# One subtraction of 2048 columns for a weight chunk's low part, in place of two of 1024

## The chip, the cores and the metric

The kernel runs on one core of a Trainium2 chip. The metric is device time in microseconds (us) of that core. Three runs of the kernel before took 1616.21, 1616.61 and 1618.96 us, median 1616.61 us.

## The reference, cut to what matters

The program computes two stacked transformer blocks on one sequence of 256 tokens of width 1024, in float32. The first block has two layers (a hybrid attention mixer, then a differential attention mixer, each followed by a convolutional gated feed-forward network). The second block has two layers, each with a three-part mixer and a mixture of 32 experts (MoE) in four groups. Nearly all work is products with weights that are each used once:

```
def conv_glu_ffn(n, w_up, conv_w, conv_b, w_down):
    gate, up = jnp.split(n @ w_up, 2, axis=-1)
    ...
    return (jax.nn.silu(conv) * up) @ w_down

def hier_moe(h, ...):
    ...
    for g in range(N_GROUPS):
        a = jnp.einsum('nd,edf->nef', t, w_gate[g])
        b = jnp.einsum('nd,edf->nef', t, w_up[g])
        hid = jax.nn.silu(a) * b * combine[:, g, :, None]
        y = y + jnp.einsum('nef,efd->nd', hid, w_down[g])
```

## The kernel before, in words

All weights come from memory as one stream of 315 chunks. A chunk is 128 partitions by 2048 float32 columns, 1 MB, and three ring places (`RING = 3`) hold it in three forms: `raw` as it arrived, `w_high` (written by ScalarE, ACT, as a rounded copy of type float32r) and `w_low` (written by VectorE, DVE, as `raw - w_high`). TensorE (PE) makes each product from three passes: high by high, high by low, low by high (lines 1225 to 1227). So every chunk goes through four hands:

- SyncE (SP) issues the transfer of chunk c into `raw` once `w_low` of chunk c-3 is finished (line 259, 260), since both ScalarE and VectorE read `raw`.
- ScalarE's `split` (lines 337 to 350) waits for the transfer and for PE to be done with chunk c-3, whose `w_high` it overwrites. Then it copies the chunk in two halves of 1024 columns, line 347, and raises `w_high_ready` after each.
- VectorE's `split` subtracts, line 701, in two halves, each behind the half of ScalarE's that it reads. After the second it raises `w_low_ready`.
- PE waits for `w_low_ready`, multiplies, and raises `chunk_used`.

Every engine works through its own list in a fixed order that is written out by hand. In the MoE (`moe`, `turn`) one expert takes three chunks: two for gate and up, one for down. VectorE's turn reads: split of the down chunk of expert e, low part of its hidden rows (line 976), split of the first up chunk of expert e+2, the hidden rows of expert e+1 (line 972), split of the second up chunk. PE's turn reads: first up chunk of e+1, two transposes of the hidden rows of e (line 1482), second up chunk, down chunk of e. PE begins the first up chunk of the next expert only when line 972 has read the bank of the expert before. A group has eight experts. At its start PE also clears sums and scatters the last group's result, and in two turns of the first three groups it gathers the next group's tokens.

In the feed-forward network (`glu`) an up chunk holds moving tiles of 256 columns, and VectorE does for each of its tiles the convolution (lines 854, 857), the gating (860) and the low part (862), between the splits. At the end of the network VectorE splits one chunk ahead before it adds PE's four banks to the residual (`add_bank`, line 835).

Of the kernel before, what the change touches and what calls it, by code (L numbers as in the profile page):

```python
# [18 lines left out]
F32 = mybir.dt.float32  # L19
F32R = mybir.dt.float32r  # L20
ALU = mybir.AluOpType
# [17 lines left out]
CH = 2048  # L39
RING = 3  # L40
# [23 lines left out]
WIDTH = {C_FB: KT * 8}  # L64
# [47 lines left out]
def build(nc, x, stream, router, small, const, fgain, out):  # L112
    es = ExitStack()
    with es:
        def sb(name, shape, dt=F32):
            return es.enter_context(nc.sbuf_tensor(name, shape, dt))
# [4 lines left out]
        raw = sb("raw", [P, RING, CH])  # L121
        wh = sb("w_high", [P, RING, CH], F32R)
        wl = sb("w_low", [P, RING, CH], F32R)
# [74 lines left out]
        w_high, w_low, chunk_used = map(sem, ("w_high_ready", "w_low_ready", "chunk_used"))  # L198
# [484 lines left out]
        def _(dve):  # L683
            step = [0]
            tt, ts, stt = nc.vector.tensor_tensor, nc.vector.tensor_scalar, nc.vector.scalar_tensor_tensor
# [6 lines left out]
            def split(c, off=0):  # L692

                if isinstance(off, int) and c + RING * off >= NCHUNK:
                    return
                u = c % RING
                n = WIDTH.get(c, CH) // 2
                for half in range(2):
                    cols = slice(half * n, half * n + n)
                    dve.wait_ge(w_high, off * (2 * RING) + (2 * c + half + 1))  # L700
                    ins = tt(wl[:, u, cols], raw[:, u, cols], wh[:, u, cols].bitcast(F32), ALU.subtract)  # L701
                ins.then_inc(w_low, 1)

            def plain(c0, n):
                for c in range(c0, c0 + n):
                    split(c + AHEAD)
# [130 lines left out]
            def out_projection(c0):  # L837
                split(c0 + AHEAD)
                split(c0 + 1 + AHEAD)
                for half in range(2):  # L840
                    add_bank(0, half, None)
                    add_bank(1, half, c0 + 2 * half + 1)
                    if half == 0:
                        split(c0 + 2 + AHEAD)
# [279 lines left out]
            for l in range(LAYERS):  # L1124
                c0 = C_LAYER[l]
                n = 8 + 5 * l
# [822 lines left out]
```

## Time and profile before

| what | value |
|---|---|
| median of three runs | 1616.61 us (1616.21 to 1618.96) |
| span of the profiled execution | 1618.9 us, the same as the slowest of the three |
| PE busy | 1532.1 us (95%) |
| weight loads (PEld) | 1292.0 us (80%) |
| VectorE busy | 1139.9 us (70%) |
| ScalarE busy | 928.7 us (57%) |
| stream read | 335.5 MB, mean of all traffic 208 GB/s |
| mean granted TensorE clock | 0.959 of full speed |

Busy shares are averages over stages. The two MoE stages lie at about 855 to 1156 us and 1308 to 1609 us, the two feed-forward networks at about 180 to 374 us and 512 to 705 us.

### The profile page before, as it was taken

The page shows a single profiled execution, that of the slowest core. Times are in us where ns is not written, and L with a number is a line of the kernel's source. Part 1 is how long each engine was busy: PE and PEld are TensorE (multiplying, and loading weights), DVE is VectorE, ACT ScalarE, POOL GpSimd, SP SyncE. Part 2 cuts the span into 40 slices and gives each one's busy share as a digit, 9 for nine tenths or more (in the row PEclk, how much of TensorE's full clock was granted, in tenths as well). Part 3 has the DMA queues.
Part 4 walks back from the last instruction along what each step waited for, and adds up shares of the span by engine and source line. Part 5 has one row for each costly group of instructions (what it writes and reads, how often), then busy time and mean ns, then how long its engine had stood idle before and what let it go on. Part 6 is the DMA issues. An engine that isn't in the chain of part 4 may idle for free.

```text
span 1618.9 us, 23376 instructions
## 1 busy us (share of the span) xinstructions
PE 1532.1 (95%) x8148; PEld 1292.0 (80%) x8148; DVE 1139.9 (70%) x1869; ACT 928.7 (57%) x1522; POOL 32.6 (2%) x68
## 2 busy tenths in 40 slices
PE   7999999999989999989979999999899799999997
PEld 5877899997868999977768888887678678888875
DVE  6554566567686656665767889889755678888886
ACT  5432445445455545455536767676555367777764
POOL 0000000000010000010000000000000000000000
PEclk9986899999999999999989999999997899999999
DMA  8510354544413454442226989798530458898884
GB/s 323 183 52 27 131 184 179 194 188 161 174 37 114 179 202 181 181 160 104 82 102 251 353 309 357 296 363 336 221 140 21 162 195 331 322 355 314 336 331 192
DMA packets 46828, 336.77 MB, mean 208 GB/s; under 512 B 5344, under 2 KB 5472, under 8 KB 6432
## 3 DMA queue, kind: packets, MB, share of 16 engines
q1 hardware_dynamic: 46656, 335.49, 54.8%
q8 instruction: 44, 0.72, 0.2%
q0 software_dynamic: 96, 0.30, 0.1%
q14 instruction: 32, 0.26, 0.0%
HBM read 334.72 MB, written 1.05 MB: 207 GB/s over the span
## 4 chain that ended last, share of the span: by engine, by line
PE 86%; DVE 6%; ACT 4%; issue 2%; POOL 1%; DMA 1%; DVEq 0%; ACTq 0%; SPq 0%; POOLq 0%
PE bank L1225 23%; PE bank L1227 23%; PE bank L1226 23%; PE bank L1327 3%; DVE w_low L701 2%; PE bank L1439 2%; PE bank L1450 2%; PE bank L1337 1%; ACT w_high L347 1%; PE bank L1273 1%; PE bank L1482 1%; PE bank L1329 1%; PE bank L1284 1%; PE bank L1348 1%; PE bank L1347 1%
## 5 line engine op out<-in xcount | busy, mean ns | idle before, releaser
L701 DVE TENSOR_TENSOR w_low<-raw,w_high 128x1024 fp32r<-128x1024 f32 (+2 forms) x630 | 734.6, 1212 | 193.2 <-ACT w_high L347 190.9
L347 ACT ACTIVATE w_high<-raw 128x1024 fp32r<-128x1024 f32 (+2 forms) x630 | 623.5, 1044 | 106.2 <-PE bank L1227 69.5
L1225 PE MATMUL bank<-w_high,x_high 128*128 128x512 f32 (+1 forms) x928 | 375.9, 405 | 8.1 <-DVE rope_b L972 3.1
L1227 PE MATMUL bank<-w_high,x_low 128*128 128x512 f32 (+1 forms) x928 | 363.7, 392 | 0.0
L1226 PE MATMUL bank<-w_low,x_high 128*128 128x512 f32 (+1 forms) x928 | 361.6, 390 | 0.0
L1225 PEld LDWEIGHTS bank<-w_high,x_high 128*128 128x128 f32 x928 | 175.5, 189 | 46.8 <-issue 7.9
L1227 PEld LDWEIGHTS bank<-w_high,x_low 128*128 128x128 f32 x928 | 175.1, 189 | 38.1
L1225 PE MATMUL bank<-x_high,w_high 128*128 128x256 f32 (+1 forms) x712 | 203.2, 285 | 0.4 <-DVE rope_b L860 0.3
L1226 PEld LDWEIGHTS bank<-w_low,x_high 128*128 128x128 f32 x928 | 176.0, 190 | 34.1 <-issue 1.4
L1226 PE MATMUL bank<-x_low,w_high 128*128 128x256 f32 (+1 forms) x712 | 202.6, 285 | 0.0
L1227 PE MATMUL bank<-x_high,w_low 128*128 128x256 f32 (+1 forms) x712 | 202.5, 284 | 0.0
L1225 PE MATMUL bank<-w_high,hid_high 128*128 128x512 f32 x432 | 171.4, 397 | 1.9 <-DVE hid_low L976 1.9
L1226 PE MATMUL bank<-w_low,hid_high 128*128 128x512 f32 x432 | 170.5, 395 | 0.0
L1227 PE MATMUL bank<-w_high,hid_low 128*128 128x512 f32 x432 | 170.4, 394 | 0.0
L1225 PEld LDWEIGHTS bank<-x_high,w_high 128*128 128x128 f32 (+1 forms) x712 | 136.8, 192 | 2.6 <-issue 1.2
L1226 PEld LDWEIGHTS bank<-x_low,w_high 128*128 128x128 f32 (+1 forms) x712 | 136.8, 192 | 1.1
L1227 PEld LDWEIGHTS bank<-x_high,w_low 128*128 128x128 f32 (+1 forms) x712 | 136.8, 192 | 0.4
L1225 PEld LDWEIGHTS bank<-w_high,hid_high 128*128 128x128 f32 x432 | 81.4, 188 | 20.1 <-DVE hid_low L976 2.3
L1227 PEld LDWEIGHTS bank<-w_high,hid_low 128*128 128x128 f32 x432 | 81.4, 189 | 19.2
L1226 PEld LDWEIGHTS bank<-w_low,hid_high 128*128 128x128 f32 x432 | 81.5, 189 | 17.5
L393 ACT ACTIVATE probs<-scores_masked,neg_max 128x128 f32<-128x128 f32 x96 | 42.8, 446 | 82.0 <-DVE neg_max L760 81.9
L495 ACT ACTIVATE hid_high<-bank 128x256 fp32r<-128x256 f32 x64 | 24.5, 383 | 80.3 <-PE bank L1482 80.3
(235 smaller groups left out, 1477.3 us busy)
## 6 DMA issues: line engine op xcount, KB each, us to landing
raw<-stream SPq DMA_DIRECT2D x314, 1024.0 KB, 4.8
const_sb<-const SPq DMA_DIRECT2D x1, 2070.0 KB, 15.1
residual<-x SPq DMA_DIRECT2D x2, 512.0 KB, 4.0
final_gain<-fgain SPq DMA_DIRECT2D x2, 512.0 KB, 10.7
out<-residual SPq DMA_DIRECT2D x2, 512.0 KB, 2.6
small_sb<-small SPq DMA_DIRECT2D x1, 765.0 KB, 6.6
rope_a<-router POOLq DMA_DIRECT2D x2, 144.0 KB, 2.5
const_sb<-const SPq DMA_DIRECT2D x1, 136.0 KB, 4.3
```

The lines of the kernel that those rows point to most:

```text
L347: nc.scalar.activation(wh[:, u, cols], raw[:, u, cols], ACT.Copy).then_inc(w_high, 1)
L393: ins = nc.scalar.activation(pr[:, a % 2, lo:hi], sm[:, a % 2, lo:hi], ACT.Exp, bias=nmax[:, a, t:t + 1], scale=-1.0, accum_out=den[:, a, ...
L495: nc.scalar.activation(gh[:, 0, :, 0:P], B[6][:, 0:2 * P].rearrange("p (k s) -> p k s", k=2), ACT.Copy)\
L701: ins = tt(wl[:, u, cols], raw[:, u, cols], wh[:, u, cols].bitcast(F32), ALU.subtract)
L1225: mm(o, ah, bh, start=start, stop=False, **kw)
L1226: mm(o, ah, bl, start=False, stop=False, **kw)
L1227: return mm(o, al, bh, start=False, stop=stop, **kw)
L1273: ins = nc.tensor.transpose(B[4 + b][:, at:at + P], tok[:, t, k * P:(k + 1) * P], ident)
L1284: ins = nc.tensor.transpose(B[4 + b][:, at:at + P], src[:, t, k * P:(k + 1) * P], ident)
L1327: ins = mm(o[:, lo:hi], q[:, t * P:(t + 1) * P], k[:, 0:hi - lo], start=True, stop=f is None)
L1439: ins = mm(B[2 + b][:, (k % 4) * P:(k % 4 + 1) * P], tok[:, t, k * P:(k + 1) * P], pick[:, t, g, :], start=t == 0, stop=t == NT - 1)
L1450: ins = mm(B[((5, 7), (2, 3))[half][t]][:, :], spread[:, g, t * P:(t + 1) * P], ys[:, half * 512:(half + 1) * 512], start=True, stop=True)
```

## The change

VectorE's `split` issues one subtraction over all columns of the chunk, behind both of ScalarE's halves, where it had issued two, each behind one half.

```
             u = c % RING
-            n = WIDTH.get(c, CH) // 2
-            for half in range(2):
-                cols = slice(half * n, half * n + n)
-                dve.wait_ge(w_high, off * (2 * RING) + (2 * c + half + 1))
-                ins = tt(wl[:, u, cols], raw[:, u, cols], wh[:, u, cols].bitcast(F32), ALU.subtract)
-            ins.then_inc(w_low, 1)
+            n = WIDTH.get(c, CH)
+            dve.wait_ge(w_high, off * (2 * RING) + (2 * c + 2))
+            tt(wl[:, u, 0:n], raw[:, u, 0:n], wh[:, u, 0:n].bitcast(F32), ALU.subtract).then_inc(w_low, 1)
```

ScalarE, PE, GpSimd and SyncE keep their lists. On VectorE nothing changes place. Line numbers behind the edit fall by two or three (701 becomes 699, 972 becomes 969).

The body of the MoE loop on VectorE (`w_low<-raw,w_high` is the split, `hid_low` the low part of the hidden rows, `rope_b<-...combine` the hidden rows), before:

```order
L701 TENSOR_TENSOR w_low<-raw,w_high 128x1024 [waits w_high_ready]
L700 REGISTER_ALU
L701 TENSOR_TENSOR w_low<-raw,w_high 128x1024 [waits w_high_ready]
L975 REGISTER_ALU
L976 TENSOR_TENSOR hid_low<-bank,hid_high 128x2x128 [waits expert_high_ready]
L700 REGISTER_ALU
L701 TENSOR_TENSOR w_low<-raw,w_high 128x1024 [waits w_high_ready]
L700 REGISTER_ALU
L701 TENSOR_TENSOR w_low<-raw,w_high 128x1024 [waits w_high_ready]
L971 REGISTER_ALU
L972 ISA [waits expert_silu_ready]
L972 SCALAR_TENSOR_TENSOR rope_b<-rope_a,combine,bank 128x256
```

And now:

```order
L699 TENSOR_TENSOR w_low<-raw,w_high 128x2048 [waits w_high_ready]
L972 REGISTER_ALU
L973 TENSOR_TENSOR hid_low<-bank,hid_high 128x2x128 [waits expert_high_ready]
L698 REGISTER_ALU
L699 TENSOR_TENSOR w_low<-raw,w_high 128x2048 [waits w_high_ready]
L968 REGISTER_ALU
L969 ISA [waits expert_silu_ready]
L969 SCALAR_TENSOR_TENSOR rope_b<-rope_a,combine,bank 128x256
```

The order of the work is the same. One instruction with one wait stands where two with a wait each stood.

The end of a feed-forward network on VectorE (`residual<-residual,bank` are the four adds), before:

```order
L701 TENSOR_TENSOR w_low<-raw,w_high 128x1024 [waits w_high_ready]
L869 REGISTER_ALU
L869 COMPARE_AND_BRANCH
L701 TENSOR_TENSOR w_low<-raw,w_high 128x1024 [waits w_high_ready] x2
L835 TENSOR_TENSOR residual<-residual,bank 128x512 [waits bank_done] x3
```

And now:

```order
L699 TENSOR_TENSOR w_low<-raw,w_high 128x2048 [waits w_high_ready]
L866 REGISTER_ALU
L866 COMPARE_AND_BRANCH
L699 TENSOR_TENSOR w_low<-raw,w_high 128x2048 [waits w_high_ready]
L832 TENSOR_TENSOR residual<-residual,bank 128x512 [waits bank_done] x3
```

The adds stand behind two chunks' splits, as before.

## Rows read from the trace of the kernel before

**Rows 1.** The page: chain that ended last, shares by engine and line; ScalarE's split.
```profile
PE 86%; DVE 6%; ACT 4%; issue 2%; POOL 1%; DMA 1%; DVEq 0%; ACTq 0%; SPq 0%; POOLq 0%
PE bank L1225 23%; PE bank L1227 23%; PE bank L1226 23%; PE bank L1327 3%; DVE w_low L701 2%; PE bank L1439 2%; PE bank L1450 2%; PE bank L1337 1%; ACT w_high L347 1%; PE bank L1273 1%; PE bank L1482 1%; PE bank L1329 1%; PE bank L1284 1%; PE bank L1348 1%; PE bank L1347 1%
...
L347 ACT ACTIVATE w_high<-raw 128x1024 fp32r<-128x1024 f32 (+2 forms) x630 | 623.5, 1044 | 106.2 <-PE bank L1227 69.5
```

**Rows 2.** Busy time by stretch: a MoE group, feed-forward network, attention; columns are named.
```profile
core 0: us, PE busy (x) PEld busy (x) DVE busy (x) ACT busy (x) POOL busy (x), PEclk, DMA share, GB/s
1016.00:1092.00 76.00, 76.00 (x352) 61.33 (x352) 67.19 (x77) 55.36 (x75) 0.00 (x0) 1.00 0.87 333
...
270.00:300.00 30.00, 30.00 (x207) 27.88 (x206) 17.71 (x26) 15.24 (x23) 0.00 (x0) 1.00 0.52 192
...
106.00:150.00 44.00, 43.14 (x139) 30.54 (x138) 13.95 (x63) 7.37 (x29) 0.00 (x0) 0.50 0.00 0
```

**Rows 3.** VectorE's groups by shape: operation, shape, count | busy us, mean ns | idle before.
```profile
L701 DVE TENSOR_TENSOR w_low<-raw,w_high 128x1024 fp32r<-128x1024 f32 x620 | 728.3, 1221 | 190.8 <-ACT w_high L347 188.5
...
L701 DVE TENSOR_TENSOR w_low<-raw,w_high 128x768 fp32r<-128x768 f32 x4 | 3.7, 954 | 2.4 <-ACT w_high L347 2.4
```

**Rows 4.** ScalarE in order of time, MoE: start us, us, engine, line, operation.
```profile
1052.09 0.39 ACT L495 ACTIVATE hid_high<-bank 128x256 fp32r<-128x256 f32 x1 [0.96 <-PE bank L1482]
1052.42 2.01 ACT L347 ACTIVATE w_high<-raw 128x1024 fp32r<-128x1024 f32 x2
...
1060.91 2.00 ACT L347 ACTIVATE w_high<-raw 128x1024 fp32r<-128x1024 f32 x2
```

**Rows 5.** VectorE in order of time, the same stretch.
```profile
1044.93 2.36 DVE L701 TENSOR_TENSOR w_low<-raw,w_high 128x1024 fp32r<-128x1024 f32 x2 [0.52 <-ACT w_high L347]
...
1053.52 2.36 DVE L701 TENSOR_TENSOR w_low<-raw,w_high 128x1024 fp32r<-128x1024 f32 x2 [0.58 <-ACT w_high L347]
1055.80 0.47 DVE L972 SCALAR_TENSOR_TENSOR rope_b<-rope_a,combine,bank 128x256 f32<-128x256 f32 x1
...
1061.99 2.36 DVE L701 TENSOR_TENSOR w_low<-raw,w_high 128x1024 fp32r<-128x1024 f32 x2 [0.52 <-ACT w_high L347]
1064.27 0.47 DVE L972 SCALAR_TENSOR_TENSOR rope_b<-rope_a,combine,bank 128x256 f32<-128x256 f32 x1
```

**Rows 6.** SyncE's queue in order of time: issues behind two splits.
```profile
1037.11 0.33 SPq L260 DMA_DIRECT2D raw<-stream  x1
...
1056.05 0.33 SPq L260 DMA_DIRECT2D raw<-stream  x1
```

**Rows 7.** Transfers of 1050 to 1062 us: issues, KB each, median us to landing.
```profile
raw<-stream SPq DMA_DIRECT2D x5, 1024.0 KB, 4.8
```

**Rows 8.** PE in order of time: start of an expert's first up chunk.
```profile
1066.00 0.40 PE L1225 MATMUL bank<-w_high,x_high 128*128 128x512 f32 x1
```

**Rows 9.** VectorE in order of time, end of the first feed-forward network.
```profile
358.19 2.36 DVE L701 TENSOR_TENSOR w_low<-raw,w_high 128x1024 fp32r<-128x1024 f32 x2 [3.50 <-ACT w_high L347]
...
367.05 4.63 DVE L701 TENSOR_TENSOR w_low<-raw,w_high 128x1024 fp32r<-128x1024 f32 x4 [0.53 <-ACT w_high L347]
371.60 2.51 DVE L835 TENSOR_TENSOR residual<-residual,bank 128x512 f32<-128x512 f32 x4
```

**Rows 10.** Chain that ended last in order of time, whole run: start us, us, what.
```profile
15.54 2.37 DVE w_low L701 x2
...
192.35 2.36 DVE w_low L701 x2
...
731.72 2.36 DVE w_low L701 x2
...
793.92 2.36 DVE w_low L701 x2
...
827.40 4.63 DVE w_low L701 x4
...
1525.33 6.41 DMA raw<-stream
```

## The prediction, made before the changed kernel ran

> **What bounds the kernel now.** I read the chain of waits first. PE holds 86% of it, the three passes 69% [rows 1], and the rest is small pieces, among them 2% on VectorE's split. So a change on VectorE matters where PE waits for it, or where it starts something that PE will wait for. Next come the stretches [rows 2]. In a feed-forward network PE is busy all 30.00 us of 30 and VectorE 17.71: much room. In the MoE PE is busy all 76.00 us of 76, VectorE 67.19, and the transfers run at 0.87 of their capacity: PE is the bound, but nothing else is far behind. Last I follow one ring place through an MoE turn in order of time, which shows what stands just behind PE.
>
> **The cost of one split.** Both kernels do the same columns. A subtraction of 1024 columns takes 1221 ns, one of 768 takes 954 ns [rows 3]: (1221 - 954) / 256 = 1.04 ns a column, and a fixed part. 2048 columns then take 1221 + 1024 x 1.04 = 2.29 us. Two halves back to back take 2.36 us [rows 5]. Where VectorE arrives late, with both of ScalarE's halves done, a split is 0.07 us shorter. The trace has no subtraction of 2048 columns. The upper bound is twice a half, 2.44 us; the lower is the slope alone, 2048 x 1.04 = 2.13 us. I take 2.29, nearest to the rows with one fixed part.
>
> Where VectorE waits for ScalarE it is the other way round. Before, ScalarE starts at 1052.42, VectorE at 1053.52 and is done at 1055.88, 3.46 us from ScalarE's start [rows 4, 5]. Of the 1.10 us between the two starts one half of ScalarE's takes 1.04 [rows 1], which leaves 0.05 for the handoff. Now VectorE starts only when both halves are written: 2.01 + 0.05 + 2.29 = 4.35 us, **0.89 us later** for `w_low`, for what stands behind it on VectorE, and for SyncE's next transfer.
>
> The Trainium skill speaks for the change here: "VectorE: DVE Perf Modes", section on the TRN2 errata, says a fixed cost is paid once per instruction, so one large tile beats several small ones. The fixed part in the rows agrees with it. By that rule alone the kernel would gain; this is the second rival below.
>
> **The MoE, by the ring place.** After a split ends at 1055.88, SyncE issues at 1056.05 (0.17) [rows 6], the transfer lands 4.8 later [rows 7], at 1060.85, ScalarE starts at 1060.91 [rows 4], VectorE at 1061.99, and it ends at 1064.35 [rows 5]. So one round of a ring place takes 0.17 + 4.8 + 0.06 + 3.44 = 8.47 us, of which 0.06 is ScalarE's idling between landing and start. PE uses three chunks per turn, and a plain turn takes 8.53 us (VectorE's splits of one ring place start at 1044.93, 1053.52 and 1061.99, half of the 17.06 between them; ScalarE's row at 1052.09 waited for PE). The ring runs just inside PE's pace. Now a round without idling takes 8.41 + 0.89 = 9.30 us: **the ring becomes the bound of every plain turn, by 9.30 - 8.53 = 0.77 us**.
>
> The first part of this is covered. The hidden rows of line 972 end at 1064.74 and PE goes on at 1066.00 [rows 5, 8]: 1.3 us of slack, less 0.1 for the semaphore's way. This is tighter than the split's own (1066.00 - 1064.35 = 1.65), because line 972 stands behind the split on VectorE and PE waits for it too. A group has eight turns. Those in which PE clears, scatters or gathers are long, and there a transfer lands well before ScalarE can use it: issued at 1037.11 [rows 6], landed near 1041.9, used 1.1 us before VectorE's 1044.93 [rows 5], so 1.9 us early. There the ring catches up, and each group starts afresh. Then come four ring-bound refills in groups one to three and five in group four. Per group: 0.89 (the first late split, still paced by PE) + 4 x 0.77 - 1.3 = 2.7 us, and in group four 0.89 + 5 x 0.77 - 1.8 (my estimate of the slack of a down chunk, which has no line 972 behind it, from the 1.65) = 2.9. Eight groups: 6 x 2.7 + 2 x 2.9 = **22 us**. Some transfers land late now and then: the chain has one of 6.41 us [rows 10], 1.6 over the median, most of which the slack took. With the slack gone it is paid. I put 1.0 us on each group of the second layer, where this row lies, an estimate between nothing and 1.6: **4 us**. MoE together 26.
>
> **The places where VectorE's split is on the chain already** [rows 10]. At 15.54 PE waits for the first chunk: +0.89. At 192.35 (start of a network, twice) the convolution stands behind the split: +0.89 each. At 731.72 (twice, one per layer) `c_tok` stands behind it: +0.89 each. At 827.40 two chunks, the second back to back: 0.89 - 0.07 = +0.8, twice. At the end of each network [rows 9] two stretches add up: the split at 358.19 is followed by the tiles, which hold up ScalarE's next chunk: +0.89; then two chunks in a row from 367.05 hold up the adds of 371.60: another +0.8. Together 1.7, twice. The four adds run without a gap, so none of them waited for PE, and PE gives no cover. At 793.92 VectorE comes late: -0.07, and a few like it, -0.3 in all. Sum: 0.9 + 1.8 + 1.8 + 1.6 + 3.4 - 0.3 = **9.2 us**.
>
> **What costs nothing.** Splits inside the networks and the projections: PE is busy throughout there, and VectorE has 12 us of 30 to spare [rows 2]. Cover gone, each would cost 0.89. SyncE's later issue hides behind those stages' slack too. VectorE's saved work, 315 x 0.07 = 22 us, is worth nothing where it waits for ScalarE, 190.8 us of idle [rows 3].
>
> **Sum.** 26 + 9.2 = 35.2 us on the profiled execution's 1618.9, so 1654.1. That execution is as long as the slowest of the three runs, 2.3 over the median; against 1616.6 the forecast is **1652 us**.
>
> **Rivals.**
> *The MoE's slack holds* (15%). The ring does not bind, because a transfer lands faster once it shares less: it would have to come down from 4.8 to about 4.1 us. For it: several are in flight at a time now. Against it: the median of the stretch is the price of every ring round there, 4.8 [rows 7], and nothing in the rows is shorter. Then only the 9.2 stay: 1626. A page of the Trainium skill, "DMA: Bandwidth & Descriptors", section on latency, says the fixed cost of a transfer shrinks when memory is less loaded, and would favour this one. No run here has shown it.
> *Faster* (4%). VectorE itself is the resource that PE waits for: 67.19 of 76 us in the MoE [rows 2]. If PE's waits come from VectorE's list being full rather than from ScalarE, each split gives back 0.07. It decides from the point where VectorE finds both halves done each time: at most 315 x 0.07 = 22, so 1595; with a third of them 1609. Against it: before almost every split of the MoE VectorE idles 0.5 us for ScalarE [rows 5].
> *The clock falls* (10%). PE would stand still about 0.76 us in a turn. In the attention the granted clock is 0.50, the 1.2 GHz level, although PE counts 43.14 us of 44 as busy [rows 2], so a high busy share is no proof of 2.4 GHz. If a tenth of the 600 us of MoE ran at 1.2 GHz, 30 us more: about 1681, with a twentieth 1666. Against it: in MoE and network the rows stand at 1.00, and PE would still have work for over 90% of a turn. The Trainium skill, "TensorE: Matmul & The Clock Gate", Part 1, makes the lower level the default that activity releases; no row shows it in the MoE.
> *The two cancel* (4%): no change that can be told.
> *As forecast* 67%. Within it, at 2.44 us a split (+0.15): 8 x 5 x 0.15 = 6 more in the ring and 2 elsewhere, 1660; at 2.13 us (-0.16) it is 1644. If late transfers are still absorbed, 1648.
>
> What a measurement can tell from no change is about 0.2%, 3.2 us. Faster 0.04, same 0.04, slower 0.92. Range 1624 to 1666: it takes in the forecast with both bounds, the first rival and the milder half of the clock case; 8% for faster and no change, 5% of the clock case and 5% for what I have not seen stay out.
>
> **What will show it.** The 2048-column subtraction at 2.29 us and VectorE's busy time down by 22 us. In the MoE: plain turns of 9.3 us and long turns unchanged; ScalarE waiting on the transfer and not on PE in the plain turns; PE waiting on line 969 (the old 972) or 699, about 0.77 us a turn once the slack is used up. A group of 76.2 us becomes about 79. Each network ends 1.7 us later. It is wrong if PE stays at 100% busy between 1016 and 1092, if transfers land in clearly less than 4.8, if the granted clock leaves 1.00 there, or if the loss falls in the networks.

## The result

| what | before | after |
|---|---|---|
| median of four runs | 1617.78 us (1616.21 to 1623.58) | 1667.83 us (1662.21 to 1671.99) |
| ratio of the times | | 1.0289, 95% interval 1.025 to 1.0328 |
| span of the profiled execution | 1618.9 | 1660.5 |
| PE busy | 1532.1 | 1547.2 |
| VectorE busy | 1139.9 | 1118.1 |
| mean granted TensorE clock | 0.959 | 0.954 |

The kernel is 2.9% slower, about 50 us, although VectorE works 21.8 us less. The forecast was 1652 (1624 to 1666), slower with 0.92. The sign and the place are right; the median lies 16 us over the forecast and 2 us over the range's end. (1.2 of the 16 us is that the kernel before itself has a median of 1617.8 here, with its fourth run, and not 1616.6.) The ratio and its interval are estimates from all the runs and differ a little from the quotient of the medians, which is 1.031; so do those of the experiments. The profiled execution of after, at 1662.21, is the shortest of its four. One run of a later kernel ("whole outside it" below) took 1931.6 us at a mean clock of 0.731, in a slow state that the others do not show, and is left out of every figure.

The page of after, the chain that ended last and ScalarE's split (answer to [rows 1]):

```profile
PE 66%; DVE 11%; DMA 10%; ACT 8%; issue 4%; POOL 1%; SPq 0%; ACTq 0%; DVEq 0%; POOLq 0%
PE bank L1222 17%; PE bank L1224 17%; PE bank L1223 17%; DMA raw<-stream 9%; DVE w_low L699 7%; ACT w_high L347 5%; PE bank L1324 2%; PE bank L1436 2%; PE bank L1447 2%; PE bank L1334 1%; PE bank L1270 1%; PE bank L1281 1%; PE bank L1326 1%; PE bank L1345 1%; PE bank L1344 1%
...
L347 ACT ACTIVATE w_high<-raw 128x1024 fp32r<-128x1024 f32 (+2 forms) x630 | 623.7, 1044 | 165.6 <-DMA raw<-stream 102.6
```

PE held 86% of the chain and now holds 66%. The other twenty per cent went to a loop of three: transfer, ScalarE's split, VectorE's split. Before this copy ScalarE used to wait mostly for PE (69.5 of 106.2 us), and now waits mostly for the transfer (102.6 of 165.6).

One MoE group and one stretch of a network (answer to [rows 2], with its columns; a group took 76.2 us, and those of after take 79.3 to 80, so the window is 79 us long):

```profile
1035.00:1114.00 79.00, 76.93 (x352) 61.02 (x351) 65.43 (x53) 56.49 (x75) 0.00 (x0) 1.00 0.85 319
287.00:317.00 30.00, 30.00 (x213) 28.21 (x212) 18.42 (x21) 13.01 (x20) 0.00 (x0) 1.00 0.58 210
```

The network's inside is unchanged, PE busy all 30 of 30. In the MoE PE now stands still for 2.07 of 79 us at a granted clock of 1.00, and the transfers' share fell from 0.87 to 0.85: no engine has a larger share of the time than before, everything waits in turn.

VectorE's subtraction by shape (answer to [rows 3]):

```profile
L699 DVE TENSOR_TENSOR w_low<-raw,w_high 128x2048 fp32r<-128x2048 f32 x310 | 707.8, 2291 | 284.7 <-ACT w_high L347 282.2
```

One operation takes 2.29 us, as estimated. It saves 21.8 us of work and gains 94 us of idle time, nearly all behind ScalarE: 284.7 us where there had been 190.8.

A plain turn of the MoE, for ScalarE, VectorE, SyncE, PE, and the median transfer (answer to [rows 4 to 8]):

```profile
1071.66 2.01 ACT L347 ACTIVATE w_high<-raw 128x1024 fp32r<-128x1024 f32 x2 [0.71 <-DMA raw<-stream]
1081.09 2.01 ACT L347 ACTIVATE w_high<-raw 128x1024 fp32r<-128x1024 f32 x2 [0.98 <-DMA raw<-stream]
```

```profile
1073.70 2.29 DVE L699 TENSOR_TENSOR w_low<-raw,w_high 128x2048 fp32r<-128x2048 f32 x1 [1.43 <-ACT w_high L347]
1075.91 0.47 DVE L969 SCALAR_TENSOR_TENSOR rope_b<-rope_a,combine,bank 128x256 f32<-128x256 f32 x1
...
1083.13 2.29 DVE L699 TENSOR_TENSOR w_low<-raw,w_high 128x2048 fp32r<-128x2048 f32 x1 [1.39 <-ACT w_high L347]
```

```profile
1076.16 0.33 SPq L260 DMA_DIRECT2D raw<-stream  x1
```

```profile
1076.44 0.50 PE L1222 MATMUL bank<-w_high,x_high 128*128 128x512 f32 x1 [0.35 <-DVE rope_b L969]
```

```profile
raw<-stream SPq DMA_DIRECT2D x4, 1024.0 KB, 4.8
```

Each of VectorE's subtractions starts 2.04 us after ScalarE's first half, not 1.10. The splits of one ring place follow each other by 1083.13 - 1073.70 = 9.43 us. PE stands still and is released by line 969, which is queued behind the split. The transfer takes 4.8 as before.

The end of the first network (answer to [rows 9]):

```profile
361.21 2.29 DVE L699 TENSOR_TENSOR w_low<-raw,w_high 128x2048 fp32r<-128x2048 f32 x1 [2.76 <-ACT w_high L347]
...
370.95 4.49 DVE L699 TENSOR_TENSOR w_low<-raw,w_high 128x2048 fp32r<-128x2048 f32 x2 [1.48 <-ACT w_high L347]
375.36 2.47 DVE L832 TENSOR_TENSOR residual<-residual,bank 128x512 f32<-128x512 f32 x4
```

From the start of the last up chunk's split to the first add it was 371.60 - 358.19 = 13.41 us; it is 14.15. The start itself lies 0.95 further behind ScalarE's (2.03 us in place of 1.08).

The chain of waits of after, in order of time, through one round of a ring place (answer to [rows 10]; start us, us, what):

```profile
1073.70 2.30 DVE w_low L699
...
1076.16 4.83 DMA raw<-stream
...
1081.09 0.08 ACT w_high L347
...
1082.06 1.05 ACT w_high L347
1083.11 0.02 issue
1083.13 2.30 DVE w_low L699
```

PE is not in it. The whole chain of after holds 31 transfers, all in the MoE; before, it held the one at 1525.33.

PE's waits by releaser (us in total, times, longest), first before:

```profile
PE bank L1225 <- DVE rope_b L972: 3.1, 3, 1.7
```

And after:

```profile
PE bank L1222 <- DVE rope_b L969: 15.9, 27, 1.7
...
PE bank L1222 <- DVE hid_low L973: 6.0, 9, 1.2
PE bank L1222 <- DVE w_low L699: 4.3, 6, 3.2
```

The wait of 3.2 us in the last line is that for the first chunk, outside the MoE.

### The profile page after: what moved, and what is told of

It reads as the page before. It is cut to its first block, busy times and chain, and to the rows that moved or that the text cites. A ratio compares the mean times of both kernels' runs of the same rounds, so it can differ in the third digit from the quotient of the medians.

```text
span 1660.5 us, 22935 instructions
## 1 busy us (share of the span) xinstructions
PE 1547.2 (93%) x8148; PEld 1293.2 (78%) x8148; DVE 1118.1 (67%) x1554; ACT 930.3 (56%) x1522; POOL 32.5 (2%) x68
## 4 chain that ended last, share of the span: by engine, by line
PE 66%; DVE 11%; DMA 10%; ACT 8%; issue 4%; POOL 1%; SPq 0%; ACTq 0%; DVEq 0%; POOLq 0%
PE bank L1222 17%; PE bank L1224 17%; PE bank L1223 17%; DMA raw<-stream 9%; DVE w_low L699 7%; ACT w_high L347 5%; PE bank L1324 2%; PE bank L1436 2%; PE bank L1447 2%; PE bank L1334 1%; PE bank L1270 1%; PE bank L1281 1%; PE bank L1326 1%; PE bank L1345 1%; PE bank L1344 1%
## 5 line engine op out<-in xcount | busy, mean ns | idle before, releaser
L699 DVE TENSOR_TENSOR w_low<-raw,w_high 128x2048 fp32r<-128x2048 f32 (+2 forms) x315 | 713.8, 2274 | 288.6 <-ACT w_high L347 286.1
L347 ACT ACTIVATE w_high<-raw 128x1024 fp32r<-128x1024 f32 (+2 forms) x630 | 623.7, 1044 | 165.6 <-DMA raw<-stream 102.6
L445 ACT ACTIVATE rope_a<-rope_a 128x256 f32<-128x256 f32 x44 | 18.4, 418 | 99.4 <-DVE rope_a L854 99.4
```

The lines of the kernel that those rows point to most:

```text
L347: nc.scalar.activation(wh[:, u, cols], raw[:, u, cols], ACT.Copy).then_inc(w_high, 1)
L445: nc.scalar.activation(gate[:, u, :], conv[:, u, :], ACT.Silu).then_inc(silu_ready, 1)
L699: tt(wl[:, u, 0:n], raw[:, u, 0:n], wh[:, u, 0:n].bitcast(F32), ALU.subtract).then_inc(w_low, 1)
```

## The experiments

The theory: what counts is the time from ScalarE's start on a chunk to the end of VectorE's subtraction. It is 0.89 us longer, which makes the ring of three places slower than PE in the MoE's plain turns and moves a few places outside it. The main rivals: the long operation itself is the cost; the cost is in proportion to the operations; the loss is TensorE's clock.

**How the runs are compared.** Every run has its span and its mean granted clock. Since the traces have no granted clock but 1.00 and 0.50, span x 2 x (1 - clock) is the time at the lower of the two levels. In 15 runs of before on one chip this goes from 110 to 150 us and the span with it, from 1610.4 to 1626.4. Within the runs of one kernel, for all kernels together, the span rises by 0.41 us for each us at the lower level (0.34 to 0.49 by kernel). The column "at equal clock" is the difference of the mean spans from before's on the same chip, less 0.41 for each us of difference in that time. Its standard error is 0.4 to 1.2, and with 0.35 or 0.47 in place of 0.41 a difference of 26 us in that time would move it by 1.6. A check of the method on the networks, below, gives 2.4 us less than their profiles do, so for the kernels with some 14 us or more at the lower level over before's the column can be that much too low. The mean of the time at the lower level has a standard error of its own, 2 to 6 us for these kernels, but 11 for the two late halves, and 2 to 3 for before.

| kernel | median us | before | ratio, 95% interval | us at the lower level (before) | at equal clock |
|---|---|---|---|---|---|
| after, again | 1667.73 | 1620.67 | 1.0290 (1.0252 to 1.0329) | 160 (134) | +35.3 |
| halves, both late | 1669.23 | 1620.67 | 1.0300 (1.0253 to 1.0346) | 148 (134) | +41.2 |
| whole in the MoE | 1653.11 | 1620.67 | 1.0189 (1.0154 to 1.0223) | 138 (134) | +29.8 |
| whole outside it | 1630.59 | 1620.67 | 1.0066 (1.0036 to 1.0096) | 151 (134) | +5.1 |
| whole in the networks | 1633.73 | 1619.33 | 1.0063 (1.0036 to 1.0091) | 148 (134) | +2.7 |
| whole for down chunks | 1634.41 | 1617.08 | 1.0096 (1.0062 to 1.0129) | 123 (128) | +19.5 |
| after, half transfers | 1655.09 | 1619.33 | 1.0190 (1.0154 to 1.0227) | 161 (134) | +19.7 |
| after, ScalarE whole too | 1670.30 | 1619.33 | 1.0283 (1.0245 to 1.0320) | 163 (134) | +34.0 |
| three parts | 1619.35 | 1619.33 | 0.9983 (0.9956 to 1.0010) | 136 (134) | -3.8 |
| four parts outside | 1616.07 | 1617.08 | 0.9989 (0.9969 to 1.0009) | 132 (128) | -3.9 |
| cut at 7/16 | 1623.80 | 1617.08 | 1.0028 (1.0002 to 1.0054) | 139 (128) | -0.5 |

**The changed kernel again.**

> The changed kernel once more, to be the measure of the next three on the same chip. Both theories: about 50 us over the kernel before, 1.025 to 1.033 of its time, as in the first comparison.

It came out so: 1.0290, 47.1 us in the medians. The whole difference of the mean spans is 46.0 us; 26 us more at the lower level account for 0.41 x 26 = 10.7 of it.

**Two operations, both late.** In the kernel before:

```
-                    dve.wait_ge(w_high, off * (2 * RING) + (2 * c + half + 1))
+                    dve.wait_ge(w_high, off * (2 * RING) + (2 * c + 2))
```

> The kernel before with one change: its two subtractions of 1024 columns both wait for ScalarE's second half. The form of the operation stays, only its start moves. Theory (latency): a split that waits for ScalarE ends 2.01 + 0.05 + 2.36 = 4.42 us after ScalarE's start, 0.07 later than in the changed kernel, so it loses all that the changed kernel loses (about 50 us) and 0.07 more in each ring-bound refill, 70 of them: 3 to 7 us above the changed kernel, 1670 to 1676. Rival (the large operation itself costs, by its length on VectorE's port or by the accesses it makes beside ScalarE's): about the kernel before, 1617 to 1625. In between, both.

Measured: 5.9 us over the changed kernel at equal clock, as the theory has it; in the medians only 1.5, at 1669.2 just under the range expected, since its runs spent less time at the lower level. The 70 refills in that expectation are about twice the 34 turns of the forecast; 0.07 in each of those is 2.4 us, with the places outside 3, and the 2.9 that are left are about what the method can be off by. In its MoE:

```profile
1072.83 2.36 DVE L701 TENSOR_TENSOR w_low<-raw,w_high 128x1024 fp32r<-128x1024 f32 x2 [1.50 <-ACT w_high L347]
```

The operations are those of before, and the loss is all there. The long operation costs nothing that could be seen by itself; the start behind the second half costs it all.

**The two halves of the change by stage.** `parts` is 1 for the chunks named and 2 for the others:

```
+                parts = 1 if of_moe(c) else 2        # the other run: not of_moe(c)
+                n = WIDTH.get(c, CH) // parts
+                for part in range(parts):
+                    cols = slice(part * n, part * n + n)
+                    dve.wait_ge(w_high, off * (2 * RING) + (2 * c + (2 if parts == 1 else part + 1)))
...
```

For the networks alone `parts` is 1 where `17 <= c < 50 or 66 <= c < 99`. The trace has 68 such subtractions and not 66: the loop's last splits, one chunk ahead, take in the chunk behind each network as well.

> One subtraction of 2048 columns for the chunks of the two MoE stages alone, two of 1024 everywhere else. Theory: the ring of three places carries the MoE's share, 28.5 us in the profiled execution of the changed kernel, and nothing moves outside: 1643 to 1648. Rival (the loss is one of TensorE's granted clock outside the MoE, set off by late chunks in the networks and the layers' starts): under 15 us here.

> The other part: one subtraction of 2048 columns for all chunks outside the two MoE stages, two of 1024 in them. Theory: the places where a split stands on the chain, 9 us by the forecast's sum, and up to 8 more where TensorE's clock comes up later at a stage's start: 1626 to 1634, and the MoE's groups stay at 76.2 us. With the run on the MoE's chunks it should add up to the changed kernel's loss within 3 us. Rival (stages act on each other through chunks loaded ahead): the sum of the two misses by more than 5.

> One subtraction of 2048 columns for the chunks of the two feed-forward networks alone (17 to 49 and 66 to 98), two of 1024 elsewhere. It splits the 12 us that the chunks outside the MoE cost. Theory: 0.89 at the start and 1.7 at the end of each network, 5.2 us, and no more time at half of TensorE's clock than in the kernel before: 1624 to 1627. Rival (the added time at the lower clock comes from the networks, whose ends let PE stand): 9 to 13 us, with the span times its mean granted clock up by only 2 to 4.

In the MoE: the medians give +32.4, and 1653.1 is 5 us over the range expected; at equal clock it is +29.8. Outside it: +9.9 in the medians, in the range, and +12.1 in the mean spans, but only 5.1 at equal clock; the other 7 are 17 us more at the lower level. In the medians the two add up to 42.3 against 47.1, 4.8 apart, outside the 3 that the theory allowed and just inside the rival's 5; in the mean spans it is 43.6 against 46.0, at equal clock 34.9 against 35.3. So nothing shows that the stages act on each other. The MoE of the kernel with whole subtractions outside only is as before, and 20 us of the layer ahead of the first MoE stand at the lower level (columns as in [rows 2]):

```profile
1040.00:1116.00 76.00, 76.00 (x353) 61.47 (x352) 67.15 (x77) 55.77 (x74) 0.00 (x0) 1.00 0.87 331
797.00:817.00 20.00, 18.94 (x85) 18.05 (x86) 9.57 (x30) 6.51 (x14) 0.00 (x0) 0.50 0.00 1
```

With the networks alone the median is 14.4 us over before's, 1633.7 where the theory had at most 1627; the mean spans differ by 8.2 us, 2.7 at equal clock. The theory was wrong in that the lower level would stay away: it takes 14 us more. The rival had 9 to 13 us and was nearly right in where the lower level comes from (14 of the 17 us, each with an error of 5). How large the waits are the profiles show by themselves. The last add before the second network and the adds at its end, before, and then in the second profile of the changed kernel:

```profile
510.26 0.69 DVE L835 TENSOR_TENSOR residual<-residual,bank 128x512 f32<-128x512 f32 x1 [2.03 <-PE bank L1227]
...
702.99 2.47 DVE L835 TENSOR_TENSOR residual<-residual,bank 128x512 f32<-128x512 f32 x4
```

```profile
509.62 0.69 DVE L832 TENSOR_TENSOR residual<-residual,bank 128x512 f32<-128x512 f32 x1 [2.03 <-PE bank L1224]
...
704.90 2.47 DVE L832 TENSOR_TENSOR residual<-residual,bank 128x512 f32<-128x512 f32 x4
```

From the end of the one to the end of the other it is 194.5 us and 197.1, both at a granted clock of 1.00. The kernel with only the networks' subtractions whole has 197.1 and 197.2 in its two networks, and every other profiled network at full clock has one of these two lengths, to 0.4 us, by its form of subtraction. So the waits cost 2.6 us in a network, 5.1 in the two, and the 2.7 at equal clock are 2.4 short of it.

**One chunk in three.** `parts = 1 if of_moe(c) and c % RING == 1`, the down chunks:

> One subtraction of 2048 columns for an expert's down chunk alone, a third of the MoE's chunks (64 of 315), two of 1024 for its up chunks and everywhere else. In the MoE the down chunk always falls to the same of the three ring places. Theory (each ring place is a round of its own, and the slowest holds up the whole turn): one late place costs nearly as much as three, 20 to 28 us: 0.87 in each of 34 plain turns, less a slack of 1.3 to 1.8 in each of 8 groups, 1638 to 1648, and ScalarE's idle time behind transfers gathers before the down chunks. Rival (cost in proportion to the operations): a third of the MoE's 30 us, 1628 to 1631.

Measured: +17.3 in the medians (1634.4, where the theory had 1638 at least and the rival 1631 at most), +19.5 at equal clock, half a us under the 20 expected. A third of the operations brings 19.5 of 29.8 us, 65%: twice its share, but not "nearly as much as three". PE's waits of this kernel:

```profile
PE bank L1231 <- DVE hid_low L982: 14.2, 22, 1.8
...
PE bank L1231 <- DVE rope_b L978: 4.1, 4, 1.7
```

PE is now released by the low part of the hidden rows, which stands behind the down chunk's split, and not by line 978, behind the up chunk's. Its first plain turns still take 8.53 and 8.53, then 8.7, 9.4, 9.2 in a group, where the changed kernel has 8.53, 9.2, 9.5, 9.5, 9.2: the slack lasts for one turn more, and once it is gone a single late place makes the turn as long as three do.

**Half the transfer.** From the changed kernel:

```
+            last_moe = (C_LAYER[1] + C_MOE) // RING
+            for lo, hi, n in ((1, last_moe, CH), (last_moe, NCHUNK // RING, CH // 2)):
+                with sync.Fori(lo, hi) as i:
+                    for u in range(RING):
+                        load(i * RING + u, u, n)
...
```

`load` moves the first `n` columns of the chunk; the kernel leaves out the other half of the weights of the second layer's MoE.

> The changed kernel, but the transfers of the second layer's MoE (chunks 219 to 314) bring 1024 of the chunk's 2048 columns; so half of those weights is left out, while every engine does the same operations. A transfer's landing there shortens by about 1 to 2 us out of 4.8. Theory (the round of a ring place is the bound): 9.30 less over 1 us is under PE's 8.53, so the second layer's MoE runs at PE's pace again, 300 to 302 us, and the first one's keeps its loss of 13 to 15: about 14 to 18 us under the changed kernel, 1648 to 1653. Rival (VectorE itself is late, because of the longer operation): nothing changes in the second layer, 1664 to 1670.

The second layer's MoE, first the row of this kernel, then that of after (1445 to 1475 us, columns as in [rows 2]), and the transfers of this kernel, 1460 to 1475 us:

```profile
1445.00:1475.00 30.00, 30.00 (x144) 24.72 (x143) 25.11 (x25) 23.02 (x31) 0.00 (x0) 1.00 0.49 161
```

```profile
1445.00:1475.00 30.00, 29.11 (x136) 23.12 (x135) 24.65 (x20) 20.98 (x29) 0.00 (x0) 1.00 0.85 318
```

```profile
raw<-stream SPq DMA_DIRECT2D x6, 512.0 KB, 3.7
```

A landing 1.1 us sooner, and in the second MoE all plain turns of PE take 8.53 to 8.55. From the first to the last of its 32 operations on the hidden rows it takes 289.1 us, 290.0 before and 304.1 in after; the first one, with the same VectorE, keeps its loss (303.7, 288.2 before and 303.4 in after). The gain over after is 15.6 us at equal clock; the median, 1655.1, lies 2 us over the range expected. So VectorE's longer operation is harmless as long as the round has room, and the 0.89 us can be paid back at another place of the round.

**ScalarE in one operation too.** From the changed kernel:

```
-                n = WIDTH.get(c, CH) // 2
-                for half in range(2):
-                    cols = slice(half * n, half * n + n)
-                    nc.scalar.activation(wh[:, u, cols], raw[:, u, cols], ACT.Copy).then_inc(w_high, 1)
+                n = WIDTH.get(c, CH)
+                nc.scalar.activation(wh[:, u, 0:n], raw[:, u, 0:n], ACT.Copy).then_inc(w_high, 2)
```

> The changed kernel with ScalarE's copy of a chunk in one operation of 2048 columns too, so that no half is left. Theory: only the time from ScalarE's start to the end of VectorE's subtraction counts; ScalarE's pair takes 2.01 us and one operation would save its fixed part, an estimate of 0.05 to 0.1 from the 1024-column operation against the pair. 70 refills by the ring and some 10 places outside, each 0.05 to 0.1 sooner: 4 to 8 us under the changed kernel, 1658 to 1663. Rival (what matters is that VectorE cannot begin with a half written): the same as the changed kernel within 2 us.

Measured: 1.3 us under the changed kernel at equal clock, with an error as large; the theory had 4 to 8. A miss, and the rival's "the same within 2 us" is what came. It does not have to be for the rival's reason, since the time from the landing hardly changed. The operation is shorter, but it starts later:

```profile
L345 ACT ACTIVATE w_high<-raw 128x2048 fp32r<-128x2048 f32 x310 | 590.0, 1912 | 170.2 <-DMA raw<-stream 75.9 <-PE bank L1222 72.3 <-issue 21.8
```

21.8 us of idle time have no releaser, 0.07 for each of 310. In the plain turns VectorE starts 1.95 after ScalarE, not 2.04, but ScalarE starts later after the landing: 0.156 and not 0.10 us for an expert's first up chunk, 0.072 and not 0.023 for the other two. Of 0.09 us 0.04 is left in a round (9.36 against 9.40), and over some 35 rounds that is 1.4; the 70 refills of the expectation were about twice as many.

**More parts.** From the kernel before, three parts on VectorE (ScalarE's copy is cut in the same way):

```
+                n = WIDTH.get(c, CH)
+                cuts = (0, n // 4, n * 9 // 16, n)
+                for part in range(3):
+                    cols = slice(cuts[part], cuts[part + 1])
+                    dve.wait_ge(w_high, off * (3 * RING) + (3 * c + part + 1))
...
```

With four parts outside the MoE the cuts lie at 5/32, 3/8 and 21/32 of the chunk; in the last kernel there are two parts with the cut at 7/16.

> The other direction: from the kernel before, ScalarE and VectorE split a chunk in three parts (512, 640 and 896 columns), each of VectorE's behind ScalarE's of the same columns. The time from ScalarE's start to the end falls from 3.46 to about 0.5 + 0.05 + 2.5 = 3.05 to 3.1 us, VectorE works 0.07 and ScalarE about 0.05 longer per chunk. Theory (the time to the end of the split is what PE waits for outside the MoE, and the ring in the MoE is PE-bound already): the places outside the MoE give back 0.4 for each 0.89 that the change cost there, 4 us, less 1 for fixed parts where VectorE comes late: 1 to 5 us under the kernel before. Rival (the fixed parts of the added operations count more): 0 to 6 us above it, with VectorE's busy time up by 20.

> From the kernel before: four parts (320, 448, 576, 704 columns) on ScalarE and VectorE for all chunks outside the two MoE stages, two halves in them. From the durations of the three-part run (512 columns 0.63 us on ScalarE, 1.04 ns a column and 0.07 per added operation on VectorE) VectorE starts 0.5 after ScalarE and is done 2.85 to 2.9 after it, against 3.46 in the kernel before and 3.23 in three parts. Theory (time to the end of the split): compared at the same time spent at TensorE's lower clock, 4 to 6 us under the kernel before, 1 to 2 under three parts: 1612 to 1617. Rival (fixed parts of the operations take over): at or above the three-part kernel's 1616 to 1619.

> From the kernel before: the cut between ScalarE's and VectorE's two parts at 7/16 (896 and 1152 columns) in place of a half. VectorE starts 0.11 sooner and both engines do as many operations as before; the split ends 0.05 to 0.1 sooner. Theory: 0.5 to 1 us under the kernel before at the same time at the lower clock, and in the time of the runs nothing that can be told: 1615 to 1621. Rival (VectorE then waits for ScalarE's longer second part, which ends 0.05 later than VectorE's first): 0 to 2 us above it.

Outside the MoE, where VectorE waits, a split ends 3.45 us after ScalarE's start in the kernel before, 4.33 in the changed one, 3.40 with the cut at 7/16, 3.22 in three parts and 3.12 in four. For four 2.9 at most was expected; VectorE starts 0.5 after ScalarE as expected, but its four operations take 2.61, where 2.29 and three times 0.07 are 2.50. Three parts give 3.8 us at equal clock, as expected; four give no more, 3.9, though 1 to 2 more were. The end of the first network in three parts shows a place where nothing is left to gain:

```profile
359.96 4.90 DVE L702 TENSOR_TENSOR w_low<-raw,w_high 128x512 fp32r<-128x512 f32 x6
364.77 1.88 DVE L836 TENSOR_TENSOR residual<-residual,bank 128x512 f32<-128x512 f32 x3
366.97 0.69 DVE L836 TENSOR_TENSOR residual<-residual,bank 128x512 f32<-128x512 f32 x1 [0.32 <-PE bank L1228]
```

The last add now waits for PE: a split that ends still sooner finds PE in its way there. From the first convolution to the end of the last add a network takes 179.5 us with two halves, with three parts and with four, so the end of the network gains nothing from more parts; its start gains 0.2 to 0.3. Whether the other places are covered in the same way was not looked at one by one. In the times themselves neither version can be told from the kernel before (both intervals hold 1), so neither is called faster. The cut at 7/16 is -0.5 at equal clock, within its error of 0.6. Its mean span is 3.9 us over before's (the interval, 1.0002 to 1.0054, just leaves out 1), and its 11 us more at the lower level account for 4.4 of that.

## Why the prediction was right, and where it was off

- *The operation of 2048 columns, 2.29 us.* Measured 2.291. VectorE's busy time fell by 21.8 us, forecast 22, worth nothing. By the Trainium skill, "VectorE: DVE Perf Modes", section on the TRN2 errata, an instruction's fixed cost is paid once; the trace agrees (2.29 us against 2.36 for the pair), and the rule was no guide to the time, as the second half's overlap was worth 0.95.
- *A split ends 0.89 later.* 3.45 to 4.33 us, +0.88.
- *The ring becomes the bound of plain turns, 9.30 against 8.53.* Right in kind, 0.1 short in size. Over the plain turns of the first MoE the round of after is 0.16 (split's end to issue) + 4.80 (transfer) + 0.10 (landing to ScalarE) + 2.04 + 2.29 + 0.01 = 9.40 us. The forecast took all of ScalarE's 0.06 as idling that would vanish; it stays, and is 0.10. The turns took 9.2 to 9.5.
- *Slack of 1.3, the late ones being line 972 behind the split.* The first late turn of a group still takes 8.53 and the next 9.2. PE's waits are on line 969, 27 times where it was 3, and on line 973, 9 times.
- *22 us, and 4 for late transfers.* The MoE alone costs 29.8 at equal clock, forecast 26. The term that was too small is the price per turn: 34 turns by 0.1 are 3.4 us. The late transfers fit, but are not shown to be 4 us: in five profiles of kernels whose three places are all late (the changed one twice, the two late halves, whole in the MoE, ScalarE whole too), the first MoE loses 13.5 to 15.8 us and the second 14.1 to 19.4, on average 3 more. In the changed kernel's first profile, though, the second loses 1.0 less than the first (14.1 and 15.1). It is the only one of the five whose second MoE has no stretch at 0.50; the others have one or two of 3.4 us, so part of the 3 us is the clock. How a late transfer works, in the kernel with whole subtractions in the MoE alone (columns as in [rows 2]; the earlier stretch stands second):

```profile
1564.30:1567.70 3.40, 3.40 (x10) 2.62 (x9) 3.35 (x2) 2.44 (x4) 0.00 (x0) 0.50 0.89 330
1560.00:1564.00 4.00, 2.12 (x9) 1.43 (x8) 3.13 (x3) 3.35 (x5) 0.00 (x0) 1.00 0.53 225
```

The transfer of chunk 293, issued at 1552.7, took 6.1 us. The same chunk's took 6.4 before [rows 10], but 4.7 and 5.1 in the two profiles of the changed kernel: which transfer is late differs from run to run. With no slack left PE stood still 1.9 of 4 us, and behind that 3.4 us were granted at 0.50. The turn took 12.2 us; before, 9.0, so most of a late transfer was indeed hidden then.
- *9.2 us outside the MoE.* The networks' 5.2 (2 x 0.89 at the start, 2 x 1.7 at the end) came out: their profiles at full clock show 0.9 at the start and 1.7 at the end, 5.1 in all. The other 4.0 were too much. At equal clock the difference between whole subtractions outside the MoE and in the networks alone is 5.1 - 2.7 = 2.4 us. So the term is about 7.5, and the 5.1 at equal clock are too low by what the method misses. The forecast took the end of a network to have no cover from PE since the adds ran without a gap; that holds for a later split, as in this change, but not for an earlier one, as the three parts show.
- *The sum, 35.2.* At equal clock the change costs 35.3. Part of this closeness is luck: the MoE's term is 3.8 too small, the other some 2 too large, and the 35.3 itself can be 2 us or more too low.
- *The clock stays.* This step failed, and it is why the median lies over the range: the sum has no term for a change in the time at the lower level, so it put it at nothing. The rival had the clock fall in the MoE, where it stays at 1.00 but for at most two such stretches of 3.4 us inside the turns. Its place is outside: the runs of after spend 160 us at the lower level against 134, about 11 us of time by the factor 0.41 and perhaps 2 less by what the networks' profiles show. It comes with the changed chunks outside the MoE (17 us) and, of these, seemingly mostly with the networks' (14), while the MoE's bring only 4; each of these has a standard error of 5, so that the 4 can be nothing, and they add up to 21 of the 26. Profiled executions show where it varies: the stretch in the first layer's attention lasts 44 to 48 or 72 us, and at the first expert layer's start there are none, 6.8 or 20.5 us. The kernel before has 10.2 us of it at the start of its first network, which takes 4.5 us longer there than the second does. Compare the same part, 785 to 805 us, in the two profiles of the changed kernel:

```profile
785.00:805.00 20.00, 19.14 (x145) 16.60 (x143) 10.99 (x49) 10.46 (x33) 0.00 (x0) 1.00 0.00 1
```

```profile
785.00:805.50 20.50, 19.43 (x89) 18.55 (x88) 10.40 (x32) 7.30 (x16) 0.00 (x0) 0.50 0.00 1
```

One and the same kernel has both. The 20.5 us stretch is also there in the three-part kernel, which is not slower. That the changed kernel spends more time at the lower level is measured; the cause stays open. Why later chunks in a network make the long stretches more frequent was not found; with one profile for nearly every kernel the runs can't show it, and no experiment here holds the clock fixed.
- *Faster, the two cancel, the MoE's slack holds.* None came. A transfer still takes 4.8. PE does wait for VectorE now, but VectorE's list is not full: it is busy 65 of 79 us in a MoE group.

## What to carry to other kernels

Where two engines hand a tile on in halves, the second half's overlap can be worth more than the instruction that a merge saves (here 0.95 against 0.07 us), if the buffer's round (use, free, transfer, convert) is close to the consumer's pace. Add up the round and compare it with the turn: the price per turn is the excess, whatever else is idle. One late place of three cost 65% of what all three did, twice its share. And a buffer ring that just fits hides its bound: the chain of the kernel before holds a single transfer, and how near the ring was to PE's pace (8.47 against 8.53 us) shows only in the sum along one place.

## What the runs showed of the hardware that was not expected

- A single ScalarE copy of 2048 columns takes 1.91 us against 2.01 for two of 1024, but begins 0.05 us later after its data landed, so over half of the 0.09 us that it saves is lost. Why was not found.
- Executions of one kernel differ by 40 us in the time at the lower clock level (110 to 150 in those of before), and each us of it goes with 0.41 us of span. In this kernel that noise (16 us between runs of before, 1% of the time) is larger than the effect of three or four parts, and only the clock beside each span makes 4 us visible.
- Transfers of 1 MB land in 4.8 us in the middle, but every profile has single ones of over 6 us, up to 7.0 in the changed kernel's first (the run's first five transfers not counted).
